# Pairs of neighbouring weight rows per partition in the load of w_gate_up, with the token rows' transposes taking every second column

## The chip, the cores and the metric

The kernel runs on one core of a Trainium2 chip, as one program in one launch. The metric is the device time of one execution in microseconds (us). The kernel before took 1235.9 us in the median of 3 runs (1235.26 to 1238.3). A change of this kernel's time of 0.3% is 3.7 us.

## The reference, cut to what matters

One layer of a streaming encoder: projections, a gated short convolution beside differential attention, a merge, a layer norm, and then a mixture of experts over 640 tokens (512 of a prompt, 128 of running streams). The change lies in the mixture of experts alone. Each token picks 2 of 32 experts; expert `e` has a 1024 x 512 matrix `w_gate_up[e]` and a 256 x 1024 matrix `w_down[e]`, all in float32:

```python
def expert_step(acc, ws):
    wgu, wd, g = ws
    a, b = jnp.split(x @ wgu, 2, axis=-1)
    return acc + g[:, None] * ((jax.nn.silu(a) * b) @ wd), None
```

`x @ wgu` is a sum over the 1024 features of a token. Any order of the 1024 terms will do, as long as the token's features and the rows of `wgu` are put in the same order.

## The kernel before

The program has four stages: `project_and_attend`, `route` (merge, norm, router, and lists of which token goes to which expert), `run_experts`, and `combine`. Each expert is one block of at most 128 token rows, so `run_experts` goes through 32 blocks `j`; a spare stretch for experts with more than 128 rows is in the program and is not entered here.

For block `j` the engines do this:

- SyncE issues the load of `w_gate_up[j]` (2 MB, line 1415) into `first_up` or `second_up`, and the load of `w_down[j]` (1 MB, line 1417) into `first_down` or `second_down`, by the parity of `j`. It issues the first when `up_lo_done` says that block `j-2` has been split completely, since the buffer is then free, and the second when `w_down[j-2]` has been split.
- GpSimd gathers the token rows of block `j` from `h_rows` with an indirect DMA (line 1430), three blocks ahead, and scatters the results of block `j-1` to `y_choice` (line 1436). Entries of a list that hold no token are out of bounds and move no row.
- TensorE turns the token rows (`turn_rows`, line 1464): 8 transposes of 128 x 128 float32. In them the token rows are the stationary operand (the weight load) and the identity is streamed.
- ScalarE and VectorE split each float32 matrix into a high and a low part in TensorE's rounded format. ScalarE casts (lines 1542 for the turned rows, 1537 for `w_down`, 1530 for `w_gate_up`), and VectorE subtracts (lines 1589, 1597, 1583). `w_gate_up` goes in 4 parts of 2 row tiles each.
- TensorE multiplies (`gate_up`, lines 1474 to 1476: 24 matmuls of 512 columns, three for each of 8 row tiles), then does the second product of the block before (`down`, lines 1495 to 1497: 12 matmuls), then turns the activations (`turn_act`, line 1484) that ScalarE (silu, line 1559) and VectorE (product, line 1603) have made.

There is one buffer for the split parts of `w_gate_up`, so part `x` of block `j+1` is cast when the matmuls of part `x` of block `j` are done. The order on each engine is written out by hand in its `body`. On ScalarE it is: turned rows of `j+1`, `w_down[j]`, three parts of `w_gate_up[j+1]`, silu of `j`, the fourth part, the copy of the result of `j-1` (line 1548), the turned activations of `j` (line 1566). On VectorE it is the same order of subtractions, with the product `act_rows` between the third and the fourth part. So a load of `w_gate_up[j+1]` that lands late holds back not only its casts but also the silu that stands behind them, and with it `act_rows` and TensorE's `turn_act`.

In the load the rows of the matrix go to partitions as `(k p) n -> p k n`: partition `p` gets rows `p`, `128 + p`, `256 + p` and so on, 8 separate rows of 512 floats (2 KB) each. `w_down` is loaded by the same rule, and its rows are 1024 floats (4 KB).

Of the kernel before, what the change touches and what calls it, by code (L numbers as in the profile page):

```python
# [32 lines left out]
P = 128  # L33
# [968 lines left out]
def route(nc, d, keep):  # L1002

    with ExitStack() as ctx:
# [5 lines left out]
        ident = const[:, C_ID:C_ID + P]  # L1010

        up, down = keep["up_raw"][0], keep["down_raw"][0]
# [39 lines left out]
        @block.sync  # L1052
        def _(sp):
            for k in range(2, KT):
                sp.dma_start(w_raw[k], d["w_out"][0, P * k:P * (k + 1), :]).then_inc(w_loaded[k], 16)
            for k in range(2, 4):
                sp.dma_start(x_rows[:, k - 2], d["x_prompt"][0, P * (k - 2):P * (k - 1), :]).then_inc(x_loaded[k - 2], 16)
            sp.dma_start(column[:], d["const"][:, C_COLUMN:C_END]).then_inc(small_in, 16)
            sp.dma_start(ln_g, d["ln1_g"].to_broadcast((P, D))).then_inc(small_in, 16)
            sp.dma_start(ln_b, d["ln1_b"].to_broadcast((P, D))).then_inc(small_in, 16)  # L1060
            sp.dma_start(b_router[:, 0:4], d["b_group"].to_broadcast((P, 4))).then_inc(small_in, 16)
            sp.dma_start(b_router[:, 4:36], d["b_router"].to_broadcast((P, 32))).then_inc(small_in, 16)
            sp.dma_start(w_router[:, :, 0:4], d["w_group"][0].rearrange("(k p) n -> p k n", p=P)).then_inc(small_in, 16)
            sp.dma_start(w_router[:, :, 4:36], d["w_router"][0].rearrange("(k p) n -> p k n", p=P)).then_inc(small_in, 16)

            def load_expert(e):
                sp.dma_start(keep["up_raw"][e][:], d["w_gate_up"][0, e].rearrange("(k p) n -> p k n", p=P)).then_inc(keep["up_in"][e], 16)
                sp.dma_start(keep["down_raw"][e][:], d["w_down"][0, e].rearrange("(k p) n -> p k n", p=P)).then_inc(keep["down_in"][e], 16)

            sp.wait_ge(split_lo, KT)  # L1070
            load_expert(0)
            for b in range(2, TB):
                src = d["x_prompt"][0, P * b:P * (b + 1), :] if b < QB else d["x_sample"].rearrange("s q d -> (s q) d")

                sp.wait_ge(taken, b - 1)
                sp.dma_start(x_rows[:, b % 2], src).then_inc(x_loaded[b % 2], 16)
            for b in range(TB - 1):
                sp.wait_ge(h_ready, 2 * (b + 1))
                sp.dma_start(d["h_rows"][P * b:P * (b + 1), :], h[:, b, :]).then_inc(h_stored[b % 2], 16)

            sp.wait_ge(h_ready, 2 * TB)
            sp.dma_start(d["h_rows"][P * (TB - 1):TOK, :], h[:, TB - 1, :]).then_inc(h_stored[(TB - 1) % 2], 16)
            load_expert(1)

            sp.dma_start(keep["ln2_g"], d["ln2_g"].to_broadcast((P, D))).then_inc(keep["ln2_in"], 16)
            sp.dma_start(keep["ln2_b"], d["ln2_b"].to_broadcast((P, D))).then_inc(keep["ln2_in"], 16)
# [247 lines left out]
def run_experts(nc, d, keep):  # L1334


    with ExitStack() as ctx:
# [4 lines left out]
        ident = const[:, C_ID:C_ID + P]  # L1342

        up_raw, down_raw, (up_hi, up_lo), (down_hi, down_lo) = keep["up_raw"], keep["down_raw"], keep["up_parts"], keep["down_parts"]
        rows, y_rows = keep["rows"], keep["y_rows"]
# [5 lines left out]
        bank_x = [pb("bank_x0"), pb("bank_x1")]  # L1351
# [4 lines left out]
        up_in, down_in, up_hi_done, up_lo_done, down_hi_done, down_lo_done = (  # L1356
            keep[n] for n in ("up_in", "down_in", "up_hi_done", "up_lo_done", "down_hi_done", "down_lo_done"))
# [42 lines left out]
        @block.sync  # L1400
        def _(sp):
            def body(j, n, par, first, last):
                if not isinstance(j, int) and keep["spare"]:
                    e = sp.value_load(eid[0:1, bass.ds(j - EXPERTS, 1)], min_val=0, max_val=EXPERTS - 1)
                elif keep["spare"]:
                    e = sp.value_load(eid[0:1, j - EXPERTS:j - EXPERTS + 1], min_val=0, max_val=EXPERTS - 1)
                else:
                    e = j if isinstance(j, int) else sp.snap(j)
                up = d["w_gate_up"][0, bass.ds(e, 1)].rearrange("a (k p) n -> p (a k) n", p=P)
                down = d["w_down"][0, bass.ds(e, 1)].rearrange("a (k p) n -> p (a k) n", p=P)  # L1410
                if isinstance(j, int) and j < 2:
                    return

                wait(sp, up_lo_done, 4 * j - 4)
                sp.dma_start(up_raw[par][:], up).then_inc(up_in[par], 16)
                wait(sp, down_lo_done, 2 * j - 2)
                sp.dma_start(down_raw[par][:], down).then_inc(down_in[par], 16)

            def stretch(j0, j1):
                keep["spare"] = j0 > 0  # L1420
                run(sp, body, j0, j1)

            all_blocks(sp, stretch, lambda: sp.wait_ge(spare_ready, 1))
# [31 lines left out]
        @block.tensor  # L1455
        def _(pe):
            def turn_rows(j, n, par):
                pe.wait_ge(rows_in[par], 16 * (n + 1))
                for half in range(2):

                    wait(pe, x_lo_done, 2 * j - 1 + half)
                    for k in range(4):
                        kk = 4 * half + k
                        last = pe.transpose(bank_x[half][:, P * k:P * (k + 1)], rows[:, par, P * kk:P * (kk + 1)], ident)
                    last.then_inc(x_turned, 1)

            def gate_up(j, par):
                pe.wait_ge(x_lo_done, 2 * j + 2)

                wait(pe, act_done, j - 1)  # L1470
                for k in range(KT):
                    if k % 2 == 0:
                        pe.wait_ge(up_lo_done, 4 * j + k // 2 + 1)
                    pe.matmul(bank_g[par][:], xT_hi[:, par, k, :], up_hi[:, k, :], start=(k == 0), stop=False)  # L1474
                    pe.matmul(bank_g[par][:], xT_hi[:, par, k, :], up_lo[:, k, :], start=False, stop=False)  # L1475
                    last = pe.matmul(bank_g[par][:], xT_lo[:, par, k, :], up_hi[:, k, :], start=False, stop=(k == KT - 1))  # L1476
                    if k % 2 == 1:
                        last.then_inc(up_used, 1)

            def turn_act(j):  # L1480
                pe.wait_ge(act_done, j + 1)
                wait(pe, a_lo_done, j)
                for k in range(2):
                    last = pe.transpose(bank_a[:, P * k:P * (k + 1)], act_rows[:, P * k:P * (k + 1)], ident)
                last.then_inc(a_turned, 1)

            def down(j, par):
                pe.wait_ge(a_lo_done, j + 1)

                wait(pe, y_taken, j)  # L1490
                for k in range(2):
                    pe.wait_ge(down_lo_done, 2 * j + k + 1)
                    for strip in range(2):
                        cols = slice(512 * strip, 512 * (strip + 1))
                        pe.matmul(bank_d[:, cols], aT_hi[:, k, :], down_hi[:, par, k, cols], start=(k == 0), stop=False)  # L1495
                        pe.matmul(bank_d[:, cols], aT_hi[:, k, :], down_lo[:, par, k, cols], start=False, stop=False)
                        last = pe.matmul(bank_d[:, cols], aT_lo[:, k, :], down_hi[:, par, k, cols], start=False, stop=(k == 1))  # L1497
                    last.then_inc(down_used, 1)

            def body(j, n, par, first, last):  # L1500
                if not last:
                    turn_rows(j + 1, n + 1 if par else n, 1 - par)
                gate_up(j, par)
                if not first:
                    down(j - 1, 1 - par)
                turn_act(j)

            def stretch(j0, j1):
                turn_rows(j0, j0 // 2, 0)
                run(pe, body, j0, j1)  # L1510
                down(j1 - 1, (j1 - 1) % 2)

            def lay_out_spare():
                pe.wait_ge(spare_laid, 1)
                for b in range(TB):
                    for n in range(2):
                        last = pe.matmul(bank_x[0][:, 0:2 * SPARE], place[:, n, b, :], of_spare[:, n, b, :],
                                         start=(b == 0 and n == 0), stop=(b == TB - 1 and n == 1))
                last.then_inc(spare_table, 1)

            all_blocks(pe, stretch, lay_out_spare)
# [337 lines left out]
```

## Time and profile before

| | |
|---|---|
| median of 3 runs | 1235.9 us |
| the profiled execution | 1238.59 us, of it the span of the profile 1236.8 us |
| mean granted TensorE clock of the span | 0.97 |
| TensorE busy | 1160.7 us, 94% of the span |
| VectorE busy | 727.5 us, 59% |
| ScalarE busy | 597.9 us, 48% |
| the experts' stage | about 863 to 1187 us in the span |

All times below are us from the start of the span. A row of the timeline gives the start of an instruction (or of several alike), its duration, engine, line, what it writes and reads, and in brackets how long the engine had been idle and what ended that. Each matmul's row overlaps the next one, since they are pipelined: their distance is the time that one costs. In a row on windows, "DMA share" is the mean busy share of the core's 16 DMA engines, which can be a little over 1, as packets overlap. A row on a DMA queue gives its packets (the small ones that set semaphores are among them), its megabytes, and the time that the packets took as a share of the 16 engines' time in the window.

### The profile page before, as it was taken

What the parts mean: (1) busy time and instruction counts of PE and PEld (TensorE: products, weight loads), DVE (VectorE), ACT (ScalarE), POOL (GpSimd) and SP (SyncE); (2) the same over time, 40 slices, a digit from 0 to 9 for tenths busy, and PEclk for the clock granted to TensorE, in tenths of its full rate; (3) what the DMA queues carried; (4) which work ended last, traced back from release to release, by engine and by line L of the source; (5) the groups of instructions that cost most, each with busy time, mean ns of one, the idle gap of its engine ahead of it and who ended that gap; (6) DMA issues with size and microseconds to landing.
All of it is one profiled execution on the core that took longest, in us unless ns stands there. A gap on an engine that the chain in (4) does not pass through costs nothing. (4 is left out here: it accounts for less than half of the span.)

```text
span 1236.8 us, 20109 instructions
## 1 busy us (share of the span) xinstructions
PE 1160.7 (94%) x7084; PEld 1016.2 (82%) x7084; DVE 727.5 (59%) x1277; ACT 597.9 (48%) x995; POOL 86.2 (7%) x91
## 2 busy tenths in 40 slices
PE   8999999999999999999889898994999999999965
PEld 8998999989989999899778897884777777777732
DVE  3325255253643536435355655556899899889927
ACT  3233433434334343344356433203788888888812
POOL 0000000000000000000000000012112121111103
PEclk9999999999999999999989998995899999999988
DMA  6525215252152521525322244624999999999724
GB/s 194 162 79 147 79 58 163 69 145 75 51 161 73 144 73 51 161 73 144 94 59 84 83 120 162 216 86 163 303 358 340 328 348 351 380 347 349 271 79 187
DMA packets 194714, 210.48 MB, mean 170 GB/s; under 512 B 14038, under 2 KB 141527, under 8 KB 194668
## 3 DMA queue, kind: packets, MB, share of 16 engines
q1 hardware_dynamic: 171680, 188.07, 46.7%
q10 hardware_dynamic: 13644, 10.77, 2.7%
q0 software_dynamic: 9344, 11.03, 2.6%
q8 instruction: 27, 0.44, 0.2%
q14 instruction: 19, 0.16, 0.0%
HBM read 200.19 MB, written 32.71 MB: 188 GB/s over the span
## 5 line engine op out<-in xcount | busy, mean ns | idle before, releaser
L344 PE MATMUL bank_u<-x_hi,w_hi 128*128 128x320 f32 (+1 forms) x1024 | 326.6, 319 | 0.4 <-DVE x_lo L763 0.4
L345 PE MATMUL bank_u<-x_lo,w_hi 128*128 128x320 f32 (+1 forms) x1024 | 318.7, 311 | 0.0
L346 PE MATMUL bank_u<-x_hi,w_lo 128*128 128x320 f32 (+1 forms) x1024 | 317.7, 310 | 0.0
L344 PEld LDWEIGHTS bank_u<-x_hi,w_hi 128*128 128x128 f32 x1024 | 192.5, 188 | 8.7 <-issue 7.1
L345 PEld LDWEIGHTS bank_u<-x_lo,w_hi 128*128 128x128 f32 x1024 | 192.9, 188 | 0.0
L346 PEld LDWEIGHTS bank_u<-x_hi,w_lo 128*128 128x128 f32 x1024 | 192.6, 188 | 0.0
L758 DVE TENSOR_TENSOR w_lo<-w_raw,w_hi 128x1024 fp32r<-128x1024 f32 x80 | 97.7, 1222 | 152.6 <-ACT w_hi L543 152.2
L543 ACT CAST w_hi<-w_raw 128x1024 fp32r<-128x1024 f32 x80 | 83.5, 1043 | 47.4 <-issue 30.2
L1474 PE MATMUL bank_g<-w_hi_space,xT_hi 128*128 128x512 f32 x256 | 103.5, 404 | 0.0
L1476 PE MATMUL bank_g<-w_hi_space,xT_lo 128*128 128x512 f32 x256 | 100.5, 392 | 0.0
L1475 PE MATMUL bank_g<-w_lo_space,xT_hi 128*128 128x512 f32 x256 | 100.3, 392 | 0.0
L618 ACT ACTIVATE prob<-bank_s,neg_max 128x512 f32<-128x512 f32 (+4 forms) x80 | 45.7, 571 | 77.5 <-DVE neg_max L852 77.3
L1583 DVE TENSOR_TENSOR w_lo_space<-second_up,w_hi_space 128x1024 fp32r<-128x1024 f32 x64 | 75.5, 1219 | 6.2 <-ACT w_hi_space L1530 6.1
L1583 DVE TENSOR_TENSOR w_lo_space<-first_up,w_hi_space 128x1024 fp32r<-128x1024 f32 x61 | 71.9, 1219 | 5.2 <-ACT w_hi_space L1530 5.1
L1530 ACT CAST w_hi_space<-second_up 128x1024 fp32r<-128x1024 f32 x64 | 64.2, 1052 | 11.4 <-DMA second_up<-in_w_gate_up 7.7
L1205 POOL TENSOR_SCALAR of_block<-const_sb,picks,choice_id 128x32 f32<-128x32 f32 x16 | 7.6, 487 | 818.5 <-DVE picks L1279 818.5
L1530 ACT CAST w_hi_space<-first_up 128x1024 fp32r<-128x1024 f32 x60 | 60.1, 1049 | 9.1 <-DMA first_up<-in_w_gate_up 8.8
L1476 PEld LDWEIGHTS bank_g<-w_hi_space,xT_lo 128*128 128x128 f32 x256 | 48.3, 189 | 10.6
L1475 PEld LDWEIGHTS bank_g<-w_lo_space,xT_hi 128*128 128x128 f32 x256 | 48.7, 190 | 9.3
L1474 PEld LDWEIGHTS bank_g<-w_hi_space,xT_hi 128*128 128x128 f32 x256 | 48.7, 190 | 9.2
L1495 PE MATMUL bank_d<-w_hi_space,aT_hi 128*128 128x512 f32 x128 | 49.9, 390 | 1.6 <-DVE aT_lo L1607 1.6
L1497 PE MATMUL bank_d<-w_hi_space,aT_lo 128*128 128x512 f32 x128 | 49.8, 389 | 0.0
(283 smaller groups left out, 2144.3 us busy)
## 6 DMA issues: line engine op xcount, KB each, us to landing
w_raw<-in_w_in SPq DMA_DIRECT2D x64, 512.0 KB, 4.1
first_up<-in_w_gate_up SPq DMA_DIRECT2D x16, 2048.0 KB
second_up<-in_w_gate_up SPq DMA_DIRECT2D x16, 2048.0 KB
first_down<-in_w_down SPq DMA_DIRECT2D x16, 1024.0 KB
second_down<-in_w_down SPq DMA_DIRECT2D x16, 1024.0 KB
k_cache<-in_cache_k SPq DMA_DIRECT2D x16, 512.0 KB
v_cache<-in_cache_v SPq DMA_DIRECT2D x16, 512.0 KB
w_raw<-in_w_branch SPq DMA_DIRECT2D x16, 512.0 KB, 4.3
```

What stands on the lines that cost most here:

```text
L344: pe.matmul(out, w_hi[:, u % 2, k, :], x_hi[:, k, cols], start=(k == 0), stop=False)
L345: pe.matmul(out, w_hi[:, u % 2, k, :], x_lo[:, k, cols], start=False, stop=False)
L346: last = pe.matmul(out, w_lo[:, u % 2, k, :], x_hi[:, k, cols], start=False, stop=(k == KT - 1))
L543: act.copy(w_hi[:, u % 2], w_raw[:, u % 2]).then_inc(s["split_hi"], 1)
L758: v.tensor_tensor(w_lo[:, u % 2], w_raw[:, u % 2], w_hi[:, u % 2].bitcast(F32), ALU.subtract).then_inc(s["split_lo"], 1)
L1474: pe.matmul(bank_g[par][:], xT_hi[:, par, k, :], up_hi[:, k, :], start=(k == 0), stop=False)
L1475: pe.matmul(bank_g[par][:], xT_hi[:, par, k, :], up_lo[:, k, :], start=False, stop=False)
L1476: last = pe.matmul(bank_g[par][:], xT_lo[:, par, k, :], up_hi[:, k, :], start=False, stop=(k == KT - 1))
L1495: pe.matmul(bank_d[:, cols], aT_hi[:, k, :], down_hi[:, par, k, cols], start=(k == 0), stop=False)
L1497: last = pe.matmul(bank_d[:, cols], aT_lo[:, k, :], down_hi[:, par, k, cols], start=False, stop=(k == 1))
L1530: act.copy(up_hi[:, 2 * x:2 * x + 2, :], up_raw[par][:, 2 * x:2 * x + 2, :]).then_inc(up_hi_done, 1)
L1583: v.tensor_tensor(up_lo[:, s, :], up_raw[par][:, s, :], up_hi[:, s, :].bitcast(F32), ALU.subtract).then_inc(up_lo_done, 1)
```

## The change

It has three edits of one kind. Both places that load `w_gate_up` (line 1067 in `route` for the first two experts, lines 1409 and 1415 in `run_experts` for the others) now give partition `p` pairs of neighbouring rows: rows `256 a + 2 p` and `256 a + 2 p + 1` for `a` from 0 to 3. The two rows lie side by side in memory and side by side in the partition, so each of the 4 pairs is one piece of 4 KB. Row tile `k = 2 a + b` of the buffer then holds rows `256 a + 2 p + b`. To match, the transpose for tile `kk` takes from the token rows the columns `256 (kk // 2) + 2 p + kk % 2`, which is every second float of a stretch of 256. The number of instructions and their order are the same on every engine; the pattern that 8 weight loads of a block read is another one, and the loads have the form 128 x 4 x 1024 instead of 128 x 8 x 512.

```diff
@@ route, load_expert
-                sp.dma_start(keep["up_raw"][e][:], d["w_gate_up"][0, e].rearrange("(k p) n -> p k n", p=P)).then_inc(keep["up_in"][e], 16)
+                sp.dma_start(keep["up_raw"][e][:].rearrange("p (a b) n -> p a (b n)", b=2), d["w_gate_up"][0, e].rearrange("(a p b) n -> p a (b n)", p=P, b=2)).then_inc(keep["up_in"][e], 16)
@@ run_experts, SyncE
-                up = d["w_gate_up"][0, bass.ds(e, 1)].rearrange("a (k p) n -> p (a k) n", p=P)
+                up = d["w_gate_up"][0, bass.ds(e, 1)].rearrange("o (a p b) n -> p (o a) (b n)", p=P, b=2)
...
-                sp.dma_start(up_raw[par][:], up).then_inc(up_in[par], 16)
+                sp.dma_start(up_raw[par][:].rearrange("p (a b) n -> p a (b n)", b=2), up).then_inc(up_in[par], 16)
@@ run_experts, TensorE, turn_rows
-                        last = pe.transpose(bank_x[half][:, P * k:P * (k + 1)], rows[:, par, P * kk:P * (kk + 1)], ident)
+                        last = pe.transpose(bank_x[half][:, P * k:P * (k + 1)], rows[:, par, 2 * P * (kk // 2):2 * P * (kk // 2 + 1)].rearrange("s (p b) -> s b p", b=2)[:, kk % 2, :], ident)
```

## Rows read from the trace of the kernel before

**Rows 1.** The page: the span in 40 slices, DMA share in tenths and GB/s.
```profile
DMA  6525215252152521525322244624999999999724
GB/s 194 162 79 147 79 58 163 69 145 75 51 161 73 144 73 51 161 73 144 94 59 84 83 120 162 216 86 163 303 358 340 328 348 351 380 347 349 271 79 187
```

**Rows 2.** Windows: length, busy us of PE, PEld, DVE, ACT, POOL; clock, DMA share, GB/s.
```profile
900.00:1200.00 300.00, 276.97 (x1322) 223.31 (x1321) 253.70 (x289) 236.96 (x311) 56.20 (x56) 0.99 0.88 315
...
1030.00:1050.00 20.00, 19.39 (x94) 15.58 (x93) 18.38 (x21) 17.06 (x23) 4.07 (x4) 1.00 1.00 349
1050.00:1070.00 20.00, 18.75 (x91) 15.02 (x91) 17.87 (x21) 16.33 (x22) 4.07 (x4) 1.00 1.00 380
```

**Rows 3.** Timeline of PE: `turn_act` of blocks 1, 18, 21, 26 and 30.
```profile
886.84 0.38 PE L1484 MATMUL bank_a<-const_sb,act_rows 128*128 128x128 f32 x2
...
1054.35 0.44 PE L1484 MATMUL bank_a<-const_sb,act_rows 128*128 128x128 f32 x2 [0.27 <-DVE act_rows L1603]
...
1085.83 0.44 PE L1484 MATMUL bank_a<-const_sb,act_rows 128*128 128x128 f32 x2 [0.52 <-DVE act_rows L1603]
...
1136.17 0.44 PE L1484 MATMUL bank_a<-const_sb,act_rows 128*128 128x128 f32 x2 [0.24 <-DVE act_rows L1603]
...
1174.95 0.44 PE L1484 MATMUL bank_a<-const_sb,act_rows 128*128 128x128 f32 x2 [0.24 <-DVE act_rows L1603]
```

**Rows 4.** Waits of 850:1200: engine, line, releaser: us in total, times, longest.
```profile
ACT w_hi_space L1530 <- DMA first_up<-in_w_gate_up: 8.8, 10, 1.5
...
ACT w_hi_space L1530 <- DMA second_up<-in_w_gate_up: 7.7, 9, 1.5
```

**Rows 5.** Timeline of a late load: ACT, DVE, then PE.
```profile
1060.09 2.95 ACT L1530 CAST w_hi_space<-first_up 128x1024 fp32r<-128x1024 f32 x3 [1.49 <-DMA first_up<-in_w_gate_up]
...
1064.58 0.41 DVE L1603 TENSOR_TENSOR act_rows<-silu,bank_g 128x256 f32<-128x256 f32 x1
...
1065.05 0.44 PE L1484 MATMUL bank_a<-const_sb,act_rows 128*128 128x128 f32 x2 [0.83 <-DVE act_rows L1603]
1065.32 1.04 PE L1464 MATMUL bank_x<-const_sb,rows 128*128 128x128 f32 x8
1066.11 0.48 PE L1474 MATMUL bank_g<-w_hi_space,xT_hi 128*128 128x512 f32 x1
```

**Rows 6.** Timeline of SyncE: issues of a load of w_gate_up and of the next two.
```profile
1006.37 0.37 SPq L1415 DMA_DIRECT2D first_up<-in_w_gate_up  x1
1011.42 0.37 SPq L1417 DMA_DIRECT2D first_down<-in_w_down  x1
1016.29 0.37 SPq L1415 DMA_DIRECT2D second_up<-in_w_gate_up  x1
```

**Rows 7.** Timeline of ACT: the casts that the load issued at 1006.37 feeds.
```profile
1019.72 2.95 ACT L1530 CAST w_hi_space<-first_up 128x1024 fp32r<-128x1024 f32 x3 [0.39 <-DMA first_up<-in_w_gate_up]
```

**Rows 8.** DMA queue 1 in four windows: 890:1170; 770:775; 1160:1163; 1019.5:1022.5.
```profile
q1 hardware_dynamic: 36731, 88.15, 87.8%
...
q1 hardware_dynamic: 550, 1.99, 100.6%
...
q1 hardware_dynamic: 495, 1.02, 92.9%
...
q1 hardware_dynamic: 443, 0.93, 96.0%
```

**Rows 9.** Groups by line, 850:1200: busy us, mean ns of one, idle before.
```profile
L1464 PE MATMUL bank_x<-const_sb,rows 128*128 128x128 f32 x256 | 36.6, 290 | 12.3 <-PEq L1004 9.5 <-issue 2.1 <-DVE xT_lo L1589 0.6
...
L1464 PEld LDWEIGHTS bank_x<-const_sb,rows 128*128 128x128 f32 x256 | 30.3, 148 | 16.0 <-issue 15.8
```

**Rows 10.** DMA issues of 890:1170: engine, count, size, us to landing.
```profile
y_choice<-y_rows,choice POOLq DMA_INDIRECT x28, 7.5
rows<-h_rows,token POOLq DMA_INDIRECT x27, 7.9
```

**Rows 11.** DMA queue 0, software, in 890:1170 and in 1062:1136: packets, MB, share.
```profile
q0 software_dynamic: 8058, 9.26, 9.2%
...
q0 software_dynamic: 2206, 3.23, 11.7%
```

## Prediction

> **What bounds the kernel now.** I read the slices of the page first, to see which stage the edited lines lie in and what is full there; then the windows of that stage, the distance between equal instructions of TensorE from block to block, the waits, one late load followed through three engines, and last the DMA queues in short windows.
>
> The slices show one stage with the DMA engines at 9 tenths, the experts' stage, at 328 to 380 GB/s; before it they are at 1 to 6 tenths [rows 1]. The windows show that two things are full at once: in 1030 to 1050 TensorE is busy 19.39 of 20 us and VectorE 18.38, and the DMA share is 1.00 [rows 2]. So a faster load can gain only what TensorE now waits.
>
> How much that is comes from the distance of one block's `turn_act` to the next one's [rows 3]. Blocks 1 to 18: (1054.35 - 886.84)/17 = 9.85 us. Blocks 18 to 21: 31.48/3 = 10.49. Blocks 21 to 26: 50.34/5 = 10.07. Blocks 26 to 30: 38.78/4 = 9.70. In the last four no cast waits for a load, so 9.70 us is what TensorE, VectorE and ScalarE need by themselves in this order. What the others have over it is 17 x 0.15 + 3 x 0.79 + 5 x 0.37 = 2.6 + 2.4 + 1.8 = 6.8 us. That is the most that faster loads can give.
>
> That the loads make this excess is in the waits: ScalarE's cast of `w_gate_up` waited 19 times for the load, 16.5 us in total [rows 4]. One case followed through: the load landed 1.49 us late, three casts began at 1060.09, the silu stood behind them, `act_rows` came at 1064.58, and TensorE stood 0.83 us before `turn_act` [rows 5]. Of 1.49 us, 0.83 reached TensorE as a wait; the rest was slack. Over the stage, 6.8 of 16.5 us reached the block distance, the same order.
>
> Why they are late: a load is issued at 1006.37 and its first cast waits until 1019.72 [rows 6, 7], 13.4 us for 2 MB, although the queue moves 2 MB in about 6 us. Behind it, `w_down` is issued at 1011.42 and the next `w_gate_up` at 1016.29 [rows 6], so there is nearly always work queued on the DMA engines, and a load waits in the queue behind the one before it. It is a limit of throughput, and the semaphore waits for the slowest of the 16 engines. Queue 0, the gathers and scatters of token rows, adds 9.2% on average, and 11.7% in the stretch in which the blocks took longest [rows 11].
>
> **The change part by part.** (1) The load of `w_gate_up` moves the same 2.10 MB in 512 packets of 4 KB instead of 1024 of 2 KB. Its price before: queue 1 moved 88.15 MB in 87.8% of 280 us, that is 245.8 us [rows 8]. A third of the bytes, 29.4 MB, is `w_down` in 4 KB packets. What 4 KB packets take is shown where nothing else runs on this queue, in 770 to 775, the load of `w_out`: 1.99 MB at 100.6% of 5 us, 396 GB/s of busy time [rows 8]. So `w_down` took 29.4/0.396 = 74 us and `w_gate_up` the other 172 us for 58.8 MB: 342 GB/s, 6.13 us for one matrix. At 396 GB/s it would be 5.30 us. The saving is 0.83 us a block in the mean over the engines.
>
> Two short windows in which queue 1 carries nearly nothing but `w_gate_up` (2.1 KB a packet in the mean) bound it. The best one, 1160 to 1163, has 1.02 MB at 92.9% of 3 us: 366 GB/s, 5.73 us for a matrix, a saving of 0.43. The worst one, 1019.5 to 1022.5, has 0.93 MB at 96.0%: 323 GB/s, 6.49 us, a saving of 1.2 [rows 8]. What differs between these two windows can't be the packets' size. If those slow spells are not a matter of size and stay, only the 0.43 or less remains. The lower end is 0, when the time goes by bytes. I take 0.6, between the best window and the mean, because the slowest engine sets the landing, and it carries the most of queue 0's packets, which the change leaves alone.
>
> What 0.6 us a block gives: the excess over 9.70 goes, in each block, by at most 0.6. The mean excess of the first 17 distances is 0.15, of the next 3 it is 0.79 and of the next 5 it is 0.37. I leave 0.2 of excess in each of the 3 (0.6 us) and 0.4 us over all the others, for single blocks above 0.6. The gain is 6.8 - 1.0 = 5.8 us.
>
> The Trainium skill, page "DMA: Bandwidth & Descriptors", section "Why small descriptors are slow (HBM only)", speaks against this size of saving: a packet costs a fixed 3 cycles or so beside its 32-byte beats, and joining packets is only worth it at 256 bytes or less. An estimate by that page: 2 x (64 + 3) = 134 cycles against 128 + 3 = 131, 2.2% of a matrix's 5.73 us or 0.13 us a block. The rows' 366 against 396 GB/s is 8%, so no row here agrees with the page's 2.2%; its case is among the rivals.
>
> (2) The first two loads, in `route`, have the same form. They are in before the stage begins, and the stage's start waits for the gather and the token rows. Nothing.
>
> (3) The issue on SyncE is one instruction as before, in the same place behind the same wait. Nothing, and no wait is added anywhere.
>
> (4) The 8 weight loads of `turn_rows` read every second float. Before, one takes 148 ns in the mean, and 8 transposes stand 0.79 us apart from first to `gate_up` (1065.32 to 1066.11) [rows 5, 9]; this lies on TensorE's own path. No row of this trace shows a weight load with a step. The bounds from these rows: nothing, or double, 0.79 us a block. I take nothing, since the nearest row is this very instruction with as many elements, and none of the rows hints at what a step costs.
>
> The Trainium skill, page "SBUF — State Buffer", in its note on cachelines, says that a read keeps full bandwidth when it takes at least two elements of each 16-byte line; a step of two float32 does. No run here shows it yet.
>
> (5) The gathers and scatters take 7.9 and 7.5 us to land [rows 10] and share the engines with the loads. If the loads leave room, they land earlier; nobody waits for them now except the buffers' reuse. Nothing.
>
> The sum: -5.8 us for the loads and 0 for the rest. The span goes from 1236.8 to 1231.0, the profiled execution's time from 1238.59 to 1232.8. That execution was 2.7 us above the median, so the median goes from 1235.9 to 1230.1; I say 1230.5, the sum rounded towards no change.
>
> **The rivals.**
>
> A, the forecast: the loads land in time in most blocks, 1228 to 1232. For it: the wait is one of throughput, and the blocks are only 0.15 to 0.8 us over their floor. Against: the slow spells may stay.
>
> B, the packet's size is nearly indifferent. The slow spells come from the memory's side or from queue 0, and the saving is 0 to 0.2 us a block. The 19 blocks whose load is late [rows 4] give at most 19 x 0.2 = 3.8 us: 1232 to 1236. For it: the 323 and 366 GB/s at one packet size. Against it: `w_out` at 396. Nearly all of it is within 0.3%. The page's 0.13 us a block would be this case (19 x 0.13 = 2.5 us).
>
> C, the stepped weight loads are slower. At double, TensorE's floor goes from 9.70 to 10.49 us a block, the loads' excess is hidden under it, and the 29 distances take 29 x 10.49 = 304.2 instead of 288.1 us, the other 2 blocks 1.6 us more: 1236 + 17.7 = about 1254. A load that is slower by a quarter costs 0.2 us a block and is even with the gain: 32 x 0.2 = 6.4. From there on the kernel is slower than before. For it: a step is untried here. Against: nothing in the rows.
>
> D, the pattern in memory is worse: each engine now steps 512 KB from one piece of 4 KB to the partition's next one, instead of 256 KB between pieces of 2 KB, and the slow spells get longer. Against it: `w_down` has this very form already, and `w_out` runs at 396 GB/s in rows of 4 KB. If it cost 0.3 us a block, 29 x 0.3 = 8.7 us: 1244.
>
> **How the numbers follow.** A 0.57, B 0.27, C 0.11, D 0.05. The range that holds 8 in 10 goes from 1227.5 (the excess goes fully and the last blocks gain a little) to 1239, which takes in all of B and the mildest part of C and D. What a measurement of this kernel can tell from no change is about 0.3%, 3.7 us, so faster means below 1232.2. A lies for the most part below it (0.5), with a little in the middle; B lies in the middle (0.27 and A's 0.07); C and D are slower, but for their mildest forms (0.14 in all): 0.52 faster, 0.34 same, 0.14 slower.
>
> **What the profile after would show.** Queue 1 with about 14,300 fewer packets in the stage and its busy share down from 87.8% to about 79% at the same length; the waits of the casts for `first_up` and `second_up` down from 16.5 us to under 4; the distance of `turn_act` over blocks 18 to 21 down from 10.49 to about 9.9 and over blocks 26 to 30 still 9.70; weight loads at line 1464 still with a mean near 148 ns. If the mean of those loads is above 180 ns, C holds. If the DMA share stays at 1.00 and the waits above 12 us, B holds. If the waits are gone and the distance is still 9.9, another loop than the one I named sets it, and the prediction is wrong in its floor of 9.70.

## The result, and the profile after

| | before | changed |
|---|---|---|
| median of 7 runs, us | 1237.89 | 1233.04 |
| lowest to highest | 1234.52 to 1238.54 | 1230.59 to 1235.13 |
| ratio of the fast runs, 95% interval | | 0.9969 [0.9954, 0.9984] |
| profiled execution / its span | 1238.59 / 1236.8 | 1232.91 / 1231.1 |
| `turn_act` to `turn_act`, mean of the 29 distances from block 1 to block 30 | 9.93 | 9.75 |
| waits of the casts of `w_gate_up` for its load | 16.5 | 2.4 |

The change takes 0.31% off, 3.8 us, with an interval of 2 to 5.7 us. The forecast was 5.8 us by its sum. The two profiled executions lie 5.7 us apart, more than the ratio says, so the two traces are good for saying which waits changed, and not for the last microsecond.

The timeline of TensorE in the changed kernel at the same blocks as in [rows 3]: start, duration, engine, line, and the wait before it.

```profile
887.12 0.38 PE L1484 MATMUL bank_a<-const_sb,act_rows 128*128 128x128 f32 x2
...
1052.61 0.44 PE L1484 MATMUL bank_a<-const_sb,act_rows 128*128 128x128 f32 x2 [0.16 <-DVE act_rows L1603]
...
1081.97 0.41 PE L1484 MATMUL bank_a<-const_sb,act_rows 128*128 128x128 f32 x2
...
1130.77 0.44 PE L1484 MATMUL bank_a<-const_sb,act_rows 128*128 128x128 f32 x2 [0.16 <-DVE act_rows L1603]
...
1169.85 0.44 PE L1484 MATMUL bank_a<-const_sb,act_rows 128*128 128x128 f32 x2 [0.16 <-DVE act_rows L1603]
```

The distances are (1052.61 - 887.12)/17 = 9.73, (1081.97 - 1052.61)/3 = 9.79, (1130.77 - 1081.97)/5 = 9.76 and (1169.85 - 1130.77)/4 = 9.77 us. Against 9.85, 10.49, 10.07 and 9.70 [rows 3] the slow stretches are gone in this execution, and the quiet one at the end is slower by 0.07. Two effects of opposite sign are at work.

The waits in 850:1200 of the changed kernel, as in [rows 4] (us in total, times, longest):

```profile
ACT w_hi_space L1530 <- DMA first_up<-in_w_gate_up: 1.5, 3, 0.6
ACT w_hi_space L1530 <- DMA second_up<-in_w_gate_up: 0.9, 3, 0.3
```

DMA queue 1 of the changed kernel in 890:1170, as the first row of [rows 8], and then in 770:775, the second row there:

```profile
q1 hardware_dynamic: 22307, 87.70, 84.7%
...
q1 hardware_dynamic: 550, 1.99, 100.6%
```

In 890:1170 it carries 14,400 packets less, as it should. But its busy time is 0.847 x 280 = 237.2 us for 87.70 MB, 2.70 us a megabyte, against 245.8/88.15 = 2.79 before. For the 3.146 MB of a block that is 8.51 instead of 8.77 us: between these two executions the queue needs 0.26 us a block less in the mean over the engines, and not 0.83 or 0.6. The figure is not exact. Among the runs below, step_only has the old load too and takes 0.891 x 260/81.40 = 2.85 us a megabyte in 890:1150, where the kernel before takes 2.79; the kernels with the new load and the old order of work lie between 2.69 and 2.71.

The weight loads of the token rows' transposes, 850:1200, as the second row of [rows 9]:

```profile
L1464 PEld LDWEIGHTS bank_x<-const_sb,rows 128*128 128x128 f32 x256 | 34.6, 209 | 15.8 <-issue 15.7
```

One takes 209 ns instead of 148. That is the second effect.

### The profile page after: what moved, and what is told of

Same layout as the page of the kernel before. It is cut to its first block and busy times, and to the rows that moved or that the text cites. A ratio compares the mean times of both kernels' runs of the same rounds, so it can differ in the third digit from the quotient of the medians.

```text
span 1231.1 us, 20109 instructions
## 1 busy us (share of the span) xinstructions
PE 1161.8 (94%) x7084; PEld 1020.6 (83%) x7084; DVE 727.1 (59%) x1277; ACT 596.2 (48%) x995; POOL 86.4 (7%) x91
## 5 line engine op out<-in xcount | busy, mean ns | idle before, releaser
L1548 ACT COPY y_rows<-bank_d 128x1024 f32<-128x1024 f32 x32 | 32.4, 1013 | 41.5 <-PE bank_d L1497 41.5
```

## The experiments

Theory T, formed from the two traces: the loads land in time, which gives about 5 to 6 us, and the stepped weight loads, which read every second float, take some 2 us of it back. The rivals are named in each expectation. All ratios are to the kernel before, run on the same chip, with 95% intervals from 5 to 12 runs of each kernel and 18 to 35 of the kernel before. "Distance" is the mean of the 29 distances of `turn_act` between blocks 1 and 30; "last four" is that of blocks 26 to 30. The waits and the weight loads are those of 850:1200. Distances, waits and weight loads come from one profiled execution of each kernel.

| run | ratio | distance | last four | waits for loads | weight load, ns |
|---|---|---|---|---|---|
| pairs_plain | 0.9973 [0.9962, 0.9983] | 9.77 | 9.70 | 6.6 | 148 |
| step_only | 1.0008 [0.9995, 1.0021] | 9.99 | 9.75 | 17.9 | 209 |
| light_plain | 0.9959 [0.9946, 0.9972] | 9.69 | 9.69 | none | 146 |
| light_step | 0.9964 [0.9951, 0.9977] | 9.74 | 9.77 | none | 209 |
| pairs_2kb | 0.9991 [0.9978, 1.0004] | 9.85 | 9.72 | 8.4 | 208 |
| pairs_4kb_two | 0.9973 [0.9961, 0.9984] | 9.76 | 9.77 | 2.4 | 209 |
| down_less | 0.9960 [0.9946, 0.9974] | 9.73 | 9.70 | 5.4 | 147 |
| quads | 0.9973 [0.9961, 0.9985] | 9.78 | 9.77 | 2.3 | 211 |
| weave_before | 0.9994 [0.9982, 1.0005] | 9.96 | 9.69 | 11.5 | 145 |
| weave_after | 0.9966 [0.9954, 0.9977] | 9.80 | 9.72 | 2.3 | 201 |
| late_before | 1.0075 [1.0058, 1.0092] | 10.31 | 9.93 | 14.6 | 145 |
| late_after | 1.0029 [1.0016, 1.0042] | 10.11 | 9.93 | 7.2 | 200 |

### The two halves of the change apart: pairs_plain and step_only

pairs_plain is the changed kernel with the plain transposes:

```diff
-rows[:, par, 2 * P * (kk // 2):2 * P * (kk // 2 + 1)].rearrange("s (p b) -> s b p", b=2)[:, kk % 2, :]
+rows[:, par, P * kk:P * (kk + 1)]
```

> The load in pairs as in the changed kernel, the transposes in plain order as in the kernel before, so the token features meet the wrong weight rows. Theory T (the faster load gives 6 us, the stepped weight loads of 209 instead of 140 ns take about 2 us back): no weight load above 150 ns in the mean, block distance 9.70, ratio to the kernel before 0.995, and 1.5 to 2 us faster than the changed kernel. Rival R1 (the stepped weight loads cost nothing at the end, since TensorE has room elsewhere): the same time as the changed kernel, ratio 0.997, block distance 9.75.

step_only is the kernel before with that edit the other way round.

> The transposes take every second column, the load is the one of the kernel before, so the token features meet the wrong weight rows. Theory T: weight loads at 209 ns, block distance up by 0.07 where no load is late and by less where one is, because a late load hides it: +0.5 to +2 us, ratio 1.0005 to 1.0015, and the casts still wait about 15 us for loads. Rival R1: no change at all, 1.0000.

The load alone gives what the whole change gives within the intervals (0.9973 and 0.9969), and the steps alone are not told from nothing by time (1.0008). By the ratio of pairs_plain R1 fares better, since T's 0.995 lies outside its interval and R1's 0.997 in it; that of step_only fits both. So the times don't show that the steps cost anything. The weight loads and the quiet stretches can tell: 148 ns and 9.70 us with plain transposes, 209 ns and 9.75 with the steps, at whichever load. The waits of step_only, in 850:1200, are those of the kernel before:

```profile
ACT w_hi_space L1530 <- DMA first_up<-in_w_gate_up: 9.6, 9, 1.6
...
ACT w_hi_space L1530 <- DMA second_up<-in_w_gate_up: 8.3, 10, 1.5
```

pairs_plain still waits 6.6 us:

```profile
ACT w_hi_space L1530 <- DMA first_up<-in_w_gate_up: 3.8, 6, 1.4
...
ACT w_hi_space L1530 <- DMA second_up<-in_w_gate_up: 2.8, 3, 1.9
```

Most of that stands in one stretch. `turn_act` of its blocks 18 and 21:

```profile
1051.22 0.44 PE L1484 MATMUL bank_a<-const_sb,act_rows 128*128 128x128 f32 x2 [0.20 <-DVE act_rows L1603]
...
1082.89 0.44 PE L1484 MATMUL bank_a<-const_sb,act_rows 128*128 128x128 f32 x2 [0.75 <-DVE act_rows L1603]
```

31.67/3 = 10.56 us, as slow as the kernel before (10.49), though the load is the new one. Blocks 1 to 18 stand at 9.68 and blocks 21 to 26 at 9.66. So the new load alone removes the late loads of most of the stage, and in this execution, the slowest of its 12, not those of blocks 18 to 21. Whether the steps keep them away in the changed kernel, or whether executions differ in this, one trace of each doesn't say.

### The floor without late loads: light_plain and light_step

```diff
-sp.dma_start(down_raw[par][:], down).then_inc(down_in[par], 16)
+sp.dma_start(down_raw[par][:, 0:1, :], down[:, 0:1, :]).then_inc(down_in[par], 16)
```

> The kernel before with only the first half of each w_down loaded from the third block on (0.5 instead of 1 MB), so no load is late; the second half is that of an older expert. Theory T: the casts wait under 1 us, block distance 9.70 over the whole stage (the floor), ratio to the kernel before 0.994 to 0.995. Rival R4 (the blocks are longer than 9.70 for another reason than late loads): the ratio stays above 0.997 and the distance above 9.8.

> The same with half of each w_down, and with the transposes taking every second column, so the token features meet the wrong weight rows. Theory T: the floor with stepped weight loads, 9.76 to 9.78 us a block, 2 us above the run that has half of each w_down and plain transposes: ratio 0.996 to 0.997. Rival R1: the same time as that run.

The waits for loads of `w_gate_up` are gone in both. `turn_act` of blocks 1, 26 and 30, first of light_plain:

```profile
885.94 0.38 PE L1484 MATMUL bank_a<-const_sb,act_rows 128*128 128x128 f32 x2
...
1128.08 0.44 PE L1484 MATMUL bank_a<-const_sb,act_rows 128*128 128x128 f32 x2 [0.20 <-DVE act_rows L1603]
...
1166.85 0.44 PE L1484 MATMUL bank_a<-const_sb,act_rows 128*128 128x128 f32 x2 [0.23 <-DVE act_rows L1603]
```

and of light_step:

```profile
885.21 0.38 PE L1484 MATMUL bank_a<-const_sb,act_rows 128*128 128x128 f32 x2
...
1128.72 0.44 PE L1484 MATMUL bank_a<-const_sb,act_rows 128*128 128x128 f32 x2 [0.16 <-DVE act_rows L1603]
...
1167.78 0.44 PE L1484 MATMUL bank_a<-const_sb,act_rows 128*128 128x128 f32 x2 [0.16 <-DVE act_rows L1603]
```

280.91/29 = 9.69 against 282.57/29 = 9.74 us. So the floor of 9.70 that the prediction read from four blocks holds for the whole stage, R4 falls, and the steps cost 0.06 us a block, 31 x 0.06 = 1.8 us by these traces. By the ratios, what late loads cost in the kernel before is 1 - 0.9959 = 0.41%, 5.1 us. The changed kernel should then gain 5.1 - 1.8 = 3.3 us, and it gained 3.8 (2 to 5.7). The 1.8 us themselves are shown by traces only; the ratios of the two runs differ by 0.0005, 0.6 us, with intervals of 0.0013 to each side. About 1 us of what is missing lies behind the experts' stage: from `turn_act` of block 30 to the end light_plain takes 62.3 us at a mean granted clock of 0.79, and light_step 61.3 at 0.84, and all five runs of light_plain have a mean clock of 0.966 or 0.967 over the span where those of light_step have 0.970 or 0.971.

Where the 0.06 comes from: in a block of the changed kernel the transposes stand 0.98 us ahead of the first product, in light_plain 0.84.

```profile
1150.92 1.23 PE L1464 MATMUL bank_x<-const_sb,rows 128*128 128x128 f32 x8 [0.20 <-issue]
1151.90 0.48 PE L1474 MATMUL bank_g<-w_hi_space,xT_hi 128*128 128x512 f32 x1
```

and light_plain:

```profile
1148.06 1.09 PE L1464 MATMUL bank_x<-const_sb,rows 128*128 128x128 f32 x8 [0.15 <-issue]
1148.90 0.48 PE L1474 MATMUL bank_g<-w_hi_space,xT_hi 128*128 128x512 f32 x1
```

Eight loads are 8 x 61 = 490 ns longer, and 140 ns of it come out on TensorE. In a block without the wait for "issue" it is 90 ns: 0.88 us (1140.82 to 1141.70 in the changed kernel) against 0.79 [rows 5]. The block's distance takes 60 ns.

### The packet or the place: pairs_2kb and pairs_4kb_two

pairs_2kb issues each load as even rows and odd rows of the same pairs:

```diff
-sp.dma_start(up_raw[par][:].rearrange("p (a b) n -> p a (b n)", b=2), up).then_inc(up_in[par], 16)
+for x in range(2):
+    sp.dma_start(up_raw[par][:].rearrange("p (a b) n -> p a b n", b=2)[:, :, x, :], up[:, :, x, :]).then_inc(up_in[par], 16)
```

> The rows go to the same partitions as in the changed kernel, but each load is two DMAs of 1 MB with packets of 2 KB, the even rows and then the odd rows; the count of packets is that of the kernel before. Theory T (the number of packets sets how late the slowest engine is): the casts wait 12 us or more for loads again, ratio to the kernel before 1.000 to 1.003. Rival R2 (which rows lie in which partition, or the addresses that engines read at the same time, matters and not the packet): the waits stay below 4 us, ratio 0.997 as the changed kernel.

pairs_4kb_two issues `a` = 0, 1 and then `a` = 2, 3, so it has two DMAs and whole pairs.

> The changed kernel with each load of w_gate_up issued as two DMAs of 1 MB, the rows of the first half of the matrix and then the second, in packets of 4 KB. It is the control of the run with two DMAs and packets of 2 KB (ratio 0.9991, waits 8.4 us). Theory T (the packet's size): ratio 0.997, waits below 4 us. Rival R7 (that run was slower than the changed kernel because of its second DMA, not its packets): ratio 0.999, waits about 8 us.

DMA queue 1 in 890:1150, and the waits, of pairs_2kb:

```profile
q1 hardware_dynamic: 34982, 82.70, 87.4%
...
ACT w_hi_space L1532 <- DMA first_up<-in_w_gate_up: 4.2, 5, 1.2
ACT w_hi_space L1532 <- DMA second_up<-in_w_gate_up: 4.2, 7, 0.9
```

and of pairs_4kb_two:

```profile
q1 hardware_dynamic: 21681, 83.58, 86.4%
...
ACT w_hi_space L1534 <- DMA first_up<-in_w_gate_up: 1.8, 4, 0.6
...
ACT w_hi_space L1534 <- DMA second_up<-in_w_gate_up: 0.6, 1, 0.6
```

The second DMA costs nothing that shows: pairs_4kb_two has the changed kernel's ratio, waits and distance, so R7 falls. With the same rows in the same partitions and two DMAs in both, 2 KB packets take 0.874 x 260/82.70 = 2.75 us a megabyte, and 4 KB packets 0.864 x 260/83.58 = 2.69. That is 2.2%, and the waits are 8.4 against 2.4 us. So the traces speak for the size of the packets, and for about half of the effect: with as many packets as the kernel before, pairs_2kb has 8.4 us of waits against 16.5, and 2.75 us a megabyte against 2.79. Whether the other half is the order of the addresses or the spread between executions, one trace of each doesn't say: three other kernels with the old load have waits of 17.9, 11.5 and 14.6 us, and pairs_plain, with packets of 4 KB, has 6.6. Nor do the ratios settle it, since their intervals overlap at 0.998. On the waits both missed, T with 12 us or more and R2 with less than 4, so R2 is neither shown nor ruled out as a part of the cause.

### How little is enough: down_less

```diff
-sp.dma_start(down_raw[par][:], down).then_inc(down_in[par], 16)
+sp.dma_start(down_raw[par][:, :, 0:928], down[:, :, 0:928]).then_inc(down_in[par], 16)
```

> The kernel before with 928 of the 1024 columns of each w_down loaded from the third block on (packets of 3.6 KB; the other columns are an older expert's), which takes 9.4% of the 2.65 us of w_down, 0.25 us a block, from the DMA engines, as much as the change took from queue 1's packets. Theory T2 (0.25 us a block in the mean over the engines is enough to let nearly every load land in time): waits of the casts for loads under 4 us, block distance 9.70 to 9.75, ratio 0.996. Rival R6 (the change helps the slowest engine by more than the mean shows, and a cut of the mean by 0.25 us does not do it): waits of 8 us or more, distance 9.80 to 9.90, ratio 0.998 to 0.999.

DMA queue 1 of down_less in 890:1150:

```profile
q1 hardware_dynamic: 34914, 81.20, 88.0%
```

That is 2.82 us a megabyte, and 8.59 us for the 3.05 MB of a block. The kernel before has 8.78 by the same window (34272 packets, 82.17 MB, 88.2%), so this run takes about 0.2 us a block away, with the old 2 KB packets and plain weight loads. The ratio is 0.9960, the distance 9.73, the waits 5.4 us. T2 holds by ratio and distance; the waits miss its 4 us. R6 falls: 0.2 us a block in the mean, here by fewer bytes and not by other packets, removes most of the loss. Blocks 18 to 21 keep a part of it, (1079.33 - 1049.23)/3 = 10.03 us.

How so little does so much is not shown by a run of its own. Two things are seen. The distance fell by 0.20 us in the mean (9.93 to 9.73) and the queue's time by 0.19, so no more was gained than was saved; the whole excess over the floor is only 9.93 - 9.69 = 0.24 us a block in the mean, though single blocks of the kernel before have 0.7 and more. And the lateness doesn't grow from load to load: SyncE issues a load when its buffer is free, and by the times of the 2 KB packets in the trace of the kernel before, the first packet follows the issue by 0.9 to 2.0 us, and this doesn't rise from one load to the next.

### Four rows: quads

The same edits with `b=4` and every fourth column, packets of 8 KB.

> Four neighbouring rows per partition, one packet of 8 KB if the queue doesn't cut it, and every fourth column in the transposes. Theory T: the load gains at most little more, since the waits are already gone; a weight load of 16-byte steps costs as much or more than the 209 ns of 8-byte steps, so 9.75 to 9.9 us a block: ratio 0.997 to 1.001. Rival R3 (the weight load is slow by its number of form dimensions, not by its step): 209 ns again, and the ratio 0.997.

The packets stay whole: queue 1 has 14367 in 890:1150, those of `w_down` among them, against 21230 in the changed kernel. It takes 0.859 x 260/83.50 = 2.67 us a megabyte, little under the 2.71 of the changed kernel in that window. The weight loads take 211 ns:

```profile
L1464 PEld LDWEIGHTS bank_x<-const_sb,rows 128*128 128x128 f32 x256 | 35.0, 211 | 16.1 <-issue 15.9
```

A step of 16 bytes costs what a step of 8 costs. R3 holds as to the number. Its reason isn't shown: the rows give one form, 128 x 128, for the plain and for both stepped loads. The time is that of the changed kernel.

### Putting the transposes behind other matmuls: weave_before and weave_after

The order of work on TensorE; the loop's bounds and the two helpers are left out:

```diff
             def body(j, n, par, first, last):
-                if not last:
+                if first:
                     turn_rows(j + 1, n + 1 if par else n, 1 - par)
                 gate_up(j, par)
-                if not first:
-                    down(j - 1, 1 - par)
+                more = not isinstance(j, int) or j + 2 < stop_at[0]
+                steps = iter(()) if first else down_steps(j - 1, 1 - par)
+                if more:
+                    turn_rows(j + 2, n + 1, par, lambda: next(steps, None))
+                for _ in steps:
+                    pass
                 turn_act(j)
```

`down_steps` is `down` with a stop after each matmul, and `turn_rows` calls its last argument ahead of each transpose.

> The kernel before with the 8 transposes of block j+2 put one by one between the 12 matmuls of the second product of block j-1, instead of together ahead of the first product. Theory T (TensorE's floor falls, and then the loads of 2 KB packets are the bound): the block distance goes from 9.9 to 9.7 or 9.8, the casts wait over 20 us for loads, ratio 0.993 to 0.998. Rival R5 (VectorE's loop is the floor): the distance is the same, ratio 1.000.

> The changed kernel with the same weaving. Theory T: each stepped weight load lies behind a matmul of 512 columns, so the 209 ns cost nothing, and the faster loads can be used: block distance 9.3 to 9.5, ratio 0.985 to 0.991 to the kernel before, and the gap between this and the woven kernel with the old load is more than the 0.3% of the change alone. Rival R5: the distance stays at 9.7, ratio 0.996.

Neither time moved: 0.9994 and 0.9966. R5 was right as to the time. The last four blocks, 9.69 and 9.72 us, hide two things, since blocks 29 and 30 of these kernels stand outside the loop and take 9.59. In blocks 12 to 18, where neither kernel waits for a load, the distance is 9.82 in both, (1051.64 - 992.74)/6 and (1049.93 - 990.99)/6. So the woven order makes a quiet block 0.1 us longer, and in it the stepped weight loads cost nothing that shows, as T had it; the rest of T missed. What the blocks lose comes back at the start, where the distance from block 0 to block 1 is 9.4 to 9.5 us instead of 11.0. ScalarE waits too, as its timeline in weave_after shows:

```profile
1138.84 1.02 ACT L1565 COPY y_rows<-bank_d 128x1024 f32<-128x1024 f32 x1 [2.12 <-PE bank_d L1503]
1139.75 0.38 ACT L1583 CAST aT_hi<-bank_a 128x256 fp32r<-128x256 f32 x1
1140.01 1.10 ACT L1559 CAST xT_hi<-bank_x 128x512 fp32r<-128x512 f32 x2
```

The copy waits for the end of the second product, and behind it stand the casts that VectorE needs for its next block. That this loop is the floor isn't shown.

### Moving that copy: late_before and late_after

ScalarE's order against that of the woven kernel:

```diff
             def body(j, n, par, first, last):
                 if not last:
                     take_rows(j + 1, 1 - par)
+                if not isinstance(j, int) or j >= begun[0] + 2:
+                    store(j - 2, par, n - 1)
                 if not isinstance(j, int) or j > 0:
                     split_down(j, n, par)
...
-                if not first:
-                    store(j - 1, 1 - par, n if par else n - 1)
                 act.wait_ge(a_turned, j + 1)
```

> The woven kernel with the old load, and on ScalarE the copy of the result of block j-2 stands after the turned rows of block j+1 instead of ahead of the turned activations, so the way from the second product to VectorE's next work is 1 us shorter. Theory T3 (the floor of 9.70 is a loop through ScalarE's copy and VectorE; take the copy out and the old loads bind): blocks without a late load 9.3 to 9.5 us, casts wait over 15 us, ratio 0.994 to 0.999. Rival R8 (TensorE's own work is the floor): distance not under 9.65 in any stretch, ratio 1.000.

> The same order of work with the changed load and stepped transposes. Theory T3: blocks of 9.4 to 9.6 us, ratio 0.990 to 0.994 to the kernel before, and at least 0.3% under the same order with the old load. Rival R8: 9.7 us, ratio 0.997.

Both expectations missed, and both kernels are slower, with 9.93 us in the last four blocks. The copy had moved from one wait of VectorE into another. VectorE in late_after, 850:1200, and one case of it:

```profile
DVE w_lo_space L1618 <- ACT w_hi_space L1554: 32.0, 30, 1.3
```

```profile
1056.06 1.29 DVE L1610 TENSOR_TENSOR xT_lo<-bank_x,xT_hi 128x512 fp32r<-128x512 f32 x2
1058.41 2.40 DVE L1618 TENSOR_TENSOR w_lo_space<-second_down,w_hi_space 128x1024 fp32r<-128x1024 f32 x2 [1.06 <-ACT w_hi_space L1554]
```

VectorE now waits 32.0/30 = 1.07 us in each block for the cast of `w_down`, which stands behind the copy. T3 missed both of its ratios and is neither shown nor ruled out as to the floor; another place for the copy wasn't tried. R8 missed too, as the distance rose. One thing is seen: in the same order of work the changed load is 0.46% ahead of the old one (1.0029 and 1.0075, intervals apart), though it carries the stepped weight loads.

No version here beats the changed kernel beyond the intervals.

## Why the prediction was right, and where its terms were not

The sign, the place and the mechanism were right, and the time lay in the range. The forecast was 1230.5 us beside a median of 1235.9; the ratio puts it at 1235.9 x 0.9969 = 1232.1, and the gain at 3.8 instead of 5.8 us. That time stands on the border between the cases A (to 1232) and B (from 1232), and does not tell them apart, nor does it tell faster from the same by the 0.3% that the prediction set (1232.2). The traces do: the waits fell to 2.4 us, where B would have had over 12.

**What bounds the kernel.** Right. Late loads were the excess over a floor of 9.70 us, which light_plain shows at 9.69 for the whole stage. Their cost was read as 6.8 us from one execution. By the ratio of light_plain it is 5.1 us (3.5 to 6.7) over many.

**Step (1), the price of the load.** The mechanism held, the price did not. The step that failed is "at 396 GB/s it would be 5.30 us": it took the rate of `w_out` in 770 to 775 for that of any 4 KB packets. The same window still shows 396 GB/s in the changed kernel, while the experts' stage, now all 4 KB, runs at 87.70/237.2 = 370. The saving was 0.26 us a block, not 0.83, and not the 0.6 that I took between mean and best window. Its split of the queue's time was right: counted packet by packet in the trace of the kernel before, 890:1150, `w_down` took 2.53 us a megabyte, 396 GB/s, and `w_gate_up` 2.91, 343 GB/s. What failed is that `w_gate_up` would come to the rate of `w_down`, and that `w_down` would keep it. In quads, where sizes still tell the two apart, `w_down` takes 2.64 and `w_gate_up` 2.68. The warning was in the text: 366 and 323 GB/s at one packet size showed that the slow spells are something else. The reason given for taking 0.6, that the slowest engine carries the most of queue 0's packets, no trace here shows, as its rows don't tell the engines apart.

The rule that the prediction weighed there, the Trainium skill's page "DMA: Bandwidth & Descriptors", section "Why small descriptors are slow (HBM only)", gave 2.2%, an estimate of 0.13 us a block. pairs_2kb and pairs_4kb_two, which send the same rows to the same partitions in two DMAs, have 2.75 and 2.69 us a megabyte, 2.2% over all of queue 1, of which `w_gate_up` is two thirds: 0.19 us a block. So in size that page of the Trainium skill was nearer than my rows. What rival B made of so small a saving is less sure: it held that 0.2 us a block gives at most 3.8 us, and down_less gained 4.9 us with 0.2, but with an interval of 3.2 to 6.7.

**What 0.6 us a block gives.** This step, "the excess over 9.70 goes, in each block, by at most 0.6", is neither confirmed nor refuted. In the changed kernel the queue needs 0.26 us a block less, and the excess of 0.79 us in blocks 18 to 21 went down to nothing over the new floor, where the step would have left 0.5 of it. But down_less left 0.33 and pairs_plain all of it. The times don't decide either: with 0.26 for 0.6 the step's own means give 17 x 0.15 + 3 x 0.26 + 5 x 0.26 = 4.6 us before the steps' cost, and pairs_plain gained 3.3 us (2.1 to 4.7).

That the time came out near is in part luck. The saving was less than half of what I took, and that mattered little, because the whole excess is 0.24 us a block in the mean, about as much as the 0.26 that was saved.

**Step (4), the stepped weight loads.** I took nothing, with bounds of nothing and 0.79 us a block. They take 209 instead of 148 ns and cost 0.06 us a block, 1.8 us. This term and the 6.8 against 5.1 us above hold the difference between 5.8 and 3.8; the 1.0 us that the forecast left standing works the other way. Rival C, "a load that is slower by a quarter costs 0.2 us a block", had the right mechanism at five times its price: the load is slower by 41%, which by that rule is 0.32 us, and 0.06 was measured, since most of it lies beside matmuls. The note on cachelines in the Trainium skill's page "SBUF — State Buffer", by which two float32 in a 16-byte line read at full bandwidth, is not what these loads show: 148 ns at step 1, 209 at step 2 (two in a line) and 211 at step 4 (one in a line). The measurement decides.

**What the profile after would show.** Packets as foretold; the queue's share 84.7% and not 79%; the waits under 4 us, as said; blocks 18 to 21 at 9.79 and not 9.9; the last four at 9.77 and not 9.70; the weight loads above the 180 ns that were to be the sign of C.

**Steps (2), (3) and (5)**, all at nothing: nothing in the traces speaks against them. The first `turn_act` stands at 876.12 against 875.85 before, and a second DMA in each load showed no cost.

## What to carry to other kernels

When a transfer is nearly always queued behind another one, compare what the change saves per period with the mean excess over the floor, and not with the worst periods: here a mean excess of 0.24 us in 9.93 was the whole prize, and 0.2 us less work of the queue took most of it. Read more than one trace, since the same load left blocks 18 to 21 at 9.79 us in one kernel and at 10.56 in another. Take the rate for a new form of a load from a stage with the same traffic beside it. And when a layout in memory is made up for by the step at which an engine reads, price that step on its own, best with the stage's transfers made light, where a cost of 0.06 us in 9.7 can be read from the trace though no ratio here shows it.

## What the runs showed of the hardware that I had not expected

- A float32 weight load of 128 x 128 of the token rows took 148 ns at step 1, 209 ns at step 2 and 211 ns at step 4, the same in every kernel to 2 ns, but for the woven order (145, and 200 to 201 ns at step 2). Of the 61 ns more, about 8 a load came out in a block's time.
- Queue 1 took 2.69 us a megabyte with packets of 4 KB and 2.75 with two thirds of its bytes in packets of 2 KB, both in two DMAs a load, and 2.67 with those two thirds in packets of 8 KB. Kernels alike in their load differed by up to 0.06 (2.79 and 2.85), so the steps between these three are small beside the spread.
- The price of a packet depended on its neighbours: the 4 KB packets of `w_down` took 2.53 us a megabyte beside 2 KB packets of `w_gate_up` and 2.64 beside packets of 8 KB.
- Behind the experts' stage executions fell into two kinds. From `turn_act` of block 30 to the end the mean granted clock was 0.84 and the time 61.8 us in the kernel before, 0.84 and 61.2 in the changed kernel, 0.84 and 61.3 in light_step, but 0.79 and 62.3 in light_plain and 0.80 and 62.6 in pairs_plain. This 1 us is none of the change's, and a ratio of whole times holds it.
